# First feed-forward program of a two-block network: its tail joined to the shifted projections without a barrier, and handed over tile by tile

## The reference, cut to what matters

```
# end of the first block
f = jnp.square(jax.nn.relu(h2 @ w_ff1)) @ w_ff2
x = x + g2 * rms_norm(f, g_post_ffn)
# start of the second block
xn = rmsnorm(x, norm1_g)
z = xn @ w_in
z_rwkv, u, gates = jnp.split(z, [SHIFT_COLS, SHIFT_COLS + SSM_WIDTH], axis=-1)
z_mix = z_rwkv + (token_shift(z_rwkv) - z_rwkv) * mu_shift
```

## Time and profile before

| what | us |
|---|---|
| median of three runs | 2864.79 |
| lowest and highest run | 2863.01, 2865.03 |
| profiled execution, its own time | 2850.7 |
| span of the profiled execution | 2848.9 |
| last matmul group of the down projection starts | 1221.75 |
| first matmul of product 0 starts | 1262.05 |
| first matmul of product 2 starts | 1283.93 |

### The profile page before, as it was taken

One profiled execution on the slowest core, in us unless ns is written; L12 is line 12 of the kernel. 1 busy time (PEld: TensorE's weight loads), 2 busy tenths in 40 slices (PEclk: granted clock), 3 DMA queues, 4 the chain that ended last, 5 costly groups with the idle time before them and its releaser, 6 DMA issues. The chain is left out here.

```text
span 2848.9 us, 42015 instructions
## 1 busy us (share of the span) xinstructions
PE 2725.7 (96%) x16814; PEld 2143.3 (75%) x16814; DVE 1876.4 (66%) x2843; ACT 1327.7 (47%) x1932; POOL 271.0 (10%) x429
## 2 busy tenths in 40 slices
PE   7999989999999999989999998989899999999998
PEld 4757644777888888867778887777778888888886
DVE  6678987567666466784777516665755476656676
ACT  4247756467555334453441104542324565543344
POOL 0115630001000000000000001210000110000000
PEclk9999999999999999999999999999999999999999
DMA  7721100446566888722463332207233666677884
GB/s 265 227 69 38 49 1 1 141 151 239 208 236 215 300 282 293 247 93 62 127 155 125 124 118 78 81 29 227 84 98 130 222 218 225 221 290 259 291 286 151
DMA packets 205906, 474.01 MB, mean 166 GB/s; under 512 B 49040, under 2 KB 69648, under 8 KB 199376
## 3 DMA queue, kind: packets, MB, share of 16 engines
q1 hardware_dynamic: 187792, 393.73, 41.7%
q0 software_dynamic: 17920, 77.61, 6.9%
HBM read 344.09 MB, written 124.29 MB: 164 GB/s over the span
## 5 line engine op out<-in xcount | busy, mean ns | idle before, releaser
L2126 PE MATMUL psum<-merged_operand 128*128 128x512 f32 x1536 | 360.7, 390 | 0.0
L2126 PEld LDWEIGHTS psum<-merged_operand 128*128 128x128 f32 x1536 | 288.4, 188 | 60.7
L2126 PE MATMUL psum<-h_half_operand 128*128 128x512 f32 x1344 | 316.8, 391 | 0.0
L2126 PEld LDWEIGHTS psum<-h_half_operand 128*128 128x128 f32 x1344 | 252.3, 188 | 55.5 <-issue 1.0
L2126 PE MATMUL psum<-h_half_operand,weight_parts_operand 128*128 128x512 f32 x768 | 177.4, 392 | 0.8 <-DVE weight_parts_operand L2615 0.6
L2126 PEld LDWEIGHTS psum<-h_half_operand,weight_parts_operand 128*128 128x128 f32 x768 | 143.5, 188 | 34.1 <-DVE weight_parts_operand L2615 2.7
L3573 PE MATMUL psum<-h_high,weight_high 128*128 128x512 f32 x480 | 151.8, 397 | 1.4 <-DVE h_low L228 1.4
L3573 PE MATMUL psum<-h_low,weight_high 128*128 128x512 f32 x480 | 148.1, 390 | 0.0
L3573 PE MATMUL psum<-h_high,weight_low 128*128 128x512 f32 x480 | 147.9, 389 | 0.0
L215 DVE CAST weight_high<-weight_ring 128x1024 fp32r<-128x1024 f32 (+1 forms) x54 | 31.7, 586 | 164.7 <-PE psum L3573 105.4
L2615 DVE TENSOR_TENSOR weight_parts_operand<-weight_ring,weight_parts_operand 128x1024 fp32r<-128x1024 f32 x66 | 80.7, 1223 | 85.0 <-ACT weight_parts_operand L2275 84.6
(11 more groups left out here) (645 smaller groups left out, 5935.0 us busy)
## 6 DMA issues: line engine op xcount, KB each, us to landing
o<-in_w_ff SPq DMA_DIRECT2D x80, 512.0 KB, 4.5
merged<-hidden_terms SPq DMA_DIRECT2D x56, 512.0 KB, 5.7
hidden_upper<-in_w_ff_down SPq DMA_DIRECT2D x48, 512.0 KB, 4.9
weight_ring<-in_w_out SPq DMA_DIRECT2D x32, 512.0 KB, 3.4
hidden_terms<-weight_parts POOLq DMA_DIRECT2D x16, 1024.0 KB, 7.9
hidden_terms<-weight_ring POOLq DMA_DIRECT2D x16, 1024.0 KB
hidden_upper<-in_w_ff_up SPq DMA_DIRECT2D x32, 512.0 KB, 4.6
o<-hidden_terms SPq DMA_DIRECT2D x28, 512.0 KB, 5.8
```

Source lines behind the costliest of these rows:

```text
L2126: mm = pe.matmul(bank, w[:, at:at + P], tiles(r, i), start=opens and m == 0, stop=closes and m == 2, skip_group_check=resumed)
```

## The change

The two functions now share one block, so there is no barrier between them, and the work at the seam is ordered anew:

- **Squares.** Of the four `Y_0E` squares DVE adds three into `acc_early`; PE sums `acc_early` and the fourth (`Y_0L`). The eight `X3_1` squares are no longer added by DVE: PE sums them one by one into bank 5. The sums of `X3_0` each have two small matmuls ahead of them (`idle=2`); the 28 and the 8 are gone.
- **PSUM.** DVE no longer copies banks 0 to 3; `add_second` of tiles 4 to 7 reads them where they are.
- **Slabs.** DVE splits slabs 0 and 1 right after the last matmul of the down projection, ahead of its wait for the root of bank 6, into the memory in which the head has them anyway.
- **Norm, rounding, rest.** These are done for each token half and tile: DVE makes `normed(half, t)`, ACT rounds it to `next_high`, DVE makes the rest into `next_low` (`rest_of_normed`), one tile behind. Half 1 comes first. The rounded tiles overwrite x, so ACT first waits until x of that half is stored (`later_x_stored`, `stored`).
- **Root of bank 7.** Its logarithm and exponential stand between the roundings of half 1, after tiles 3 and 5.
- **Products.** PE runs products 0 and 1 together (`first_two`): for each half and tile three matmuls for slab 0, and three for slab 1 one tile behind. From product 2 on nothing changes.

```diff
 if first:
-    sum_acc(5, acc_late, 2 * KT + 3 * OUTS)
-    sum_squares(7, X3_0)
-    K.stay_busy(pe, 4, 28)
+    sum_squares(5, X3_1)
+    sum_squares(7, X3_0, idle=2)
...
-    load_log_table(1)
-    wait(act, sq_summed, 2 * KT + OUTS)
-    root((root_x_down[:, halves[0]], 7))
+    wait(act, later_x_stored, 16)
+    for t in range(KT):
+        round_normed(1, t, t)
+        if t == 3:
+            wait(act, sq_summed, 3 * KT + 1)
+            log_of(root_x_down[:, halves[0]], 7)
+        if t == 5:
+            root_of(root_x_down[:, halves[0]])
+    wait(act, stored, 16 * KT)
+    for t in range(KT):
+        round_normed(0, t, KT + t)
...
-    for t in range(OUTS):
-        wait(dve, sq_made, begin[Y_0E] + t + 1)
-        dve.tensor_copy(tiles(y21, t), psum[:, t, :]).then_inc(c_added.sem, 1)
-    for t in range(KT):
-        add_square(X3_1, t, acc_late, t == 0)
-    wait(dve, c_added, 4 * OUTS)
+    for t in range(OUTS - 1):
+        add_square(Y_0E, t, acc_early, False)
+    wait(dve, tile_ended, tiles_by[STEPS - 1])
+    split_next_w(0)
+    split_next_w(1)
     wait_root(6)
     for t in range(KT):
         add_second(0, t, 3 * KT + t)
-    wait_root(7)
     wait(dve, dw_split, STEPS)
     wait(dve, dh_split, STEPS)
-    for t in range(KT):
-        normed(1, t)
-    wait_root(8)
-    for t in range(KT):
-        normed(0, t)
+    for half, root_at in ((1, 7), (0, 8)):
+        wait_root(root_at)
+        for t in range(KT + 1):
+            if t < KT:
+                normed(half, t)
+            if t:
+                rest_of_normed(half, t - 1, (1 - half) * KT + t - 1)
...
+def part_of_half(n, g, k):
+    cols = slice(k * P, (k + 1) * P)
+    whi, wlo = w_ahead[n]
+    for m, (w, x) in enumerate(((whi, high), (whi, low), (wlo, high))):
+        mm = pe.matmul(banks(n)[:, g, :], w[:, cols], x[:, k, at(g)],
+                       start=(k == 0 and m == 0), stop=(k == KT - 1 and m == 2))
+    if g == 0 and k == KT - 1:
+        mm.then_inc(K.slab_used.sem, 1)
+def first_two():
+    pe.wait_ge(K.slab_split.sem, split0 + 2)
+    for g in (1, 0):
+        for k in range(KT + 1):
+            if k < KT:
+                pe.wait_ge(K.tile_split.sem, tile0 + (1 - g) * KT + k + 1)
+                part_of_half(0, g, k)
+            if k:
+                part_of_half(1, g, k - 1)
...
-    K.stay_busy(pe, 7, 8)
+    first_two()
     for n in range(N):
-        product(n)
+        if n >= 2:
+            product(n)
```

More of the change, by code:

```diff
@@ L1698, in attend, with mix_and_ffn @@
             f.n += n
-def mix_and_ffn(nc, K, x_twin, room_twin, hid_twin, weights, x_from, w_up, w_down, gain, bias, first, x_dram, kept, out=None):
+def mix_and_ffn(nc, K, x_twin, room_twin, hid_twin, weights, x_from, w_up, w_down, gain, bias, first, x_dram, kept, out=None, shared_block=None):
     OUTS, MIX, PAIRS, STEPS = 4, 2 * KT, FT // 2, 56
@@ L1729, in mix_and_ffn @@
     if first:
-        SQUARES = [("PE", KT), ("DVE", KT), ("DVE", OUTS), ("DVE", OUTS), ("DVE", OUTS), ("DVE", KT), ("PE", OUTS), ("PE", KT)]
-        X2_0, X2_1, Y_0A, Y_1A, Y_1B, X3_1, Y_0E, X3_0 = range(8)
+        SQUARES = [("PE", KT), ("DVE", KT), ("DVE", OUTS), ("DVE", OUTS), ("DVE", OUTS), ("PE", KT), ("DVE", OUTS - 1), ("PE", 1),
+                   ("PE", KT)]
+        X2_0, X2_1, Y_0A, Y_1A, Y_1B, X3_1, Y_0E, Y_0L, X3_0 = range(9)
     else:
@@ L1740, in mix_and_ffn @@
             takers.append((who, counts[who]))
+    if first:
+        takers[begin[Y_0L]] = ("PE", KT + 1)
+        takers[begin[X3_1]:begin[X3_1] + KT] = [("PE", KT + 2 + t) for t in range(KT)]
     order = []
@@ L1861, in bank_b @@
             return psum[:, (2, 7)[i % 2], :]
+        loaded_next = [at + sum(16 if n < MIX else 32 for n in range(slot, SLABS, RING)) for slot, at in enumerate(loaded0)]
         def landed(n):
@@ L1911, in residual, with next_high, next_low, next_w @@
             return x[:, t, halves[h]]
-        with nc.Block() as block:
+        NORMED, AHEAD = OPERANDS + 5 + STEPS, SLABS + 2 * PAIRS + STEPS
+        def next_high(h, t):
+            return x_operand[:, t, halves[h]]
+        def next_low(h, t):
+            return hid_operand[:, 2 * t + h, :]
+        def next_w(n):
+            at = slice(n * KT * P, (n + 1) * KT * P)
+            return pair_high[:, 0:4 * HALF][:, at], pair_high[:, 4 * HALF:8 * HALF][:, at]
+        ahead_of_next = [next_w(n) for n in range(2)] if first else None
+        with nc.Block() if shared_block is None else nullcontext(shared_block) as block:
             @block.sync
@@ L2114, in sum_acc, with sum_squares @@
                     sum_of(bank, of).then_inc(summed.sem, 1)
-                def sum_squares(bank, group, begins=True):
+                def sum_squares(bank, group, begins=True, idle=0):
                     many = SQUARES[group][1]
@@ L2257, in load_log_table, with log_of, root_of, root @@
                     act.activation(K.silu_c[:, n:n + 1], K.col("eps"), ACT.Ln)
[L2259 to L2263, removed]
-                    wait(act, log_made, len(logs))
-                    for to, _ in which:
-                        act.activation(to, to, ACT.Exp, scale=-0.5).then_inc(root_made.sem, 1)
+                def log_of(to, bank):
+                    logs.append(to)
+                    act.activation(to, psum[:, bank, :], ACT.Ln, scale=1.0 / D, bias=K.col("eps")).then_inc(log_made.sem, 1)
+                def root_of(to):
+                    wait(act, log_made, len(logs))
+                    act.activation(to, to, ACT.Exp, scale=-0.5).then_inc(root_made.sem, 1)
+                def root(which):
+                    log_of(*which)
+                    root_of(which[0])
+                def round_normed(h, t, count):
+                    wait(act, h_made, 2 * KT + count + 1)
+                    act.activation(next_high(h, t), hid_b[:, 2 * t + h, :], ACT.Copy).then_inc(pair_rounded.sem, 1)
                 def round_source(half, k):
@@ L3396, in _ @@
                                                    op1=ALU.add))
-                split_w(0)
-                for k in range(KT):
-                    rest_of_tile(dve, K, xhigh0, k, normed, high, low)
-                split_w(1)
                 dve.wait_ge(K.load_done.sem, load0 + 32)
```

102 lines of the change are left out of this document (59 added, 43 removed).

## The result

In the first comparison the changed kernel took 2842.1 us (median of four runs, 2839.9 to 2849.8) against 2863.9 us of the kernel before (four runs, 2861.9 to 2865.0). The ratio of the times is 0.9947, 95% interval 0.9929 to 0.9964. So it is faster, as forecast; but 2842.1 lies under the range of 2851 to 2859, and the 21.8 us between the medians are nearly twice the 11.6 us of the sum. The two profiles show 2848.9 and 2838.5 us of span, which is 10.4 us. Before asking where further microseconds came from, the seam can be checked step by step.

A forecast was written before the change was run, and what follows sets the result against it. PE, busy 96% of the span, was taken as the bound; products 0 and 1 end 13.8 us earlier, 2.2 go back: 2850.7 - 11.6 = 2839.1 us, plus 14.1 to the runs' median gives 2853.2, range 2851.0 to 2859.0.

The forecast's parts named there:

- the sum: Whole seam: products 0 and 1 end 13.8 us earlier, 2.2 us go back, so product 2 starts 11.6 us sooner.
- The runs' median stands 14.1 us above that execution: Whole kernel: 14.1 us from profiled execution to runs' median, used to turn 2839.1 us into 2853.2 us.
- additions start: DVE's `add_second` at the seam: starts 2.3 us sooner, 5.2 us after the last down matmul, not 7.5.
- first product: PE at the seam: starts at once after the last `X3_0` sum, at 1248.3 on the old profile's clock.
- DVE's waits for ACT: Half 1 of norms and rests: logarithm and exponential of the root stall DVE by 0.7 and 0.5 us.
- idle ahead of product 2: PE between products 0 and 1 and product 2: 2.2 us idle, where it had none.
- PE was said to set its own start: Square sums ahead of the first product: PE itself is the wait; fillers cost at most 1.8 us.
- the clock rival: Low clock stretch on matmuls at the seam costs 1.5 to 3 us; time 2855 to 2856 us; chance 0.22.
- signs of being wrong: `first_two` starting after 1250 or over 24 us, gap over 4 us ahead of product 2, or changed time after it.
- what follows it is unchanged and moves with it: Everything after product 2's start: takes the same time as before, only shifted with that start.
- The hand-over: Tiles passing DVE, ACT, DVE, PE: up to 3.2 us exposed; 2856 to 2857 us; chance 0.14 together with tables.
- A switch of tables: ACT's root: 1.31 us a switch; rival form, twice that, gives 2856.8 us; chance 0.14 together with hand-over.

The follow-up runs named there:

- a lag of three: Changed kernel with product 1 three tiles behind product 0 instead of one; mean 2845.0 us over 11 executions, product 2 after 50.88 us.
- late splits: Changed kernel with the splits of slabs 0 and 1 behind the additions to x and ahead of the norms; mean 2848.7 us, product 2 after 54.58 us.

## Why the prediction was right and wrong

**The step that failed** is the last sentence of the sum: "The runs' median stands 14.1 us above that execution; taking the gain off it gives 2853.2 us", and with it "the median itself moves by about 1". The 14.1 us are no fixed distance between a profiled execution and a run. Over 86 later executions the kernel before spread from 2846.9 to 2864.9 us, with the granted clock: the profiled one lies at the low end of that, the three runs at the high end (their clocks are not on record). The mean of the 86 is 2856.5 us, 5.8 us above the profiled one; 2856.5 - 11.6 is 2844.9, and the changed kernel's mean over 20 is 2845.5. With the shown median as an anchor the forecast was 8.3 us too high. The other 2.8 us down to the measured 2842.1 are the four executions of the changed kernel, which lay 3.4 us under the mean of the 20, against 0.6 us by which that mean is above 2844.9. The three runs lay within 2 us of each other, and the profile's own time stood 14 us below: that contradiction was in the times shown, and should have widened the range downward. The 21.8 us of the first comparison are the same effect: 11.0, and 7.4 by which the kernel before's median was above its later mean, and 3.4 by which the changed one's was below. 11.0 us, give or take 2.1, is the size over all executions, 11.4 the seam. One thing is not explained: all four executions of the kernel before in the first comparison took 2861.9 us or more, and only 6 of the 86 later ones did. As four independent draws that would be very rare, so something that no run here shows may have held them up.

**The steps of the seam**, forecast and measured, each from the last 24 down matmuls:

| step | forecast | measured |
|---|---|---|
| additions start | 10.9 | 10.91 |
| first norm | 22.9 | 22.90 |
| first product | 26.6 | 26.17 |
| DVE's waits for ACT | 0.7, 0.5, none | 0.69, 0.36, 0.38 |
| idle ahead of product 2 | 2.2 | 2.07 |
| product 2 | 50.6 | 50.80 |

The first product was in truth as late as forecast. Its record starts at 1246.99 while the last sum, started at 1246.53 and 0.86 us long, is still under way until 1247.39, which is 26.6 us after the down matmuls; the product's second matmul starts at 1247.63. From there to the last start at 1269.17 it is 21.5 us for 94 steps, 0.2 us more than at 0.227 each. Most of that is one wait for a tile (the pair at 1258.77 takes 0.78 us, its neighbours 0.62), and it follows the third wait for ACT, which the forecast did not have. Product 2 is 0.2 us late by it.

**PE was said to set its own start.** It does, but that was worth nothing: without fillers it starts 0.69 us sooner and product 2 doesn't move, because PE then waits for tiles. PE is nowhere more than about 1.5 us behind DVE's tile, and at 1258.77 it has caught up. The runs with a lag of three and with late splits show the other side of that: there DVE set the pace.

**The rivals.** The clock did not drop between the down matmuls and product 2 in any of the three profiles of the changed kernel. But right behind the gap of 2.07 us it fell in one of the three, on matmuls, and cost 1.6 us, which is what the clock rival said (1.5 to 3 us). The forecast and this rival thus both occur, from execution to execution; neither explains the miss, which has the other sign. Of the prediction's signs of being wrong one came true, the changed time behind product 2 (1.9 us in the first pair of profiles): "what follows it is unchanged and moves with it" holds for the instructions, not for their time. The clock did matter for the whole: the spread follows it, and the fillers, which the forecast costed at up to 1.8 us of loss, go with a gain of 5.3 us, give or take 2.5. The hand-over was hidden nearly as forecast: 1.4 us of waits on DVE, about 0.2 us of them on PE. A switch of tables cost 1.30 us (1248.52 to 1249.82) and no more. The Trainium skill, "ScalarE: Activation LUTs", section "What ACT_TABLE_LOAD costs", says about 2.66 us with the drain, and this trace disagrees. The barrier's removal by itself was not tried, since the barrier keeps the reused memory apart.

**What stays open.** Why the executions differ in their clock at all, and why without the fillers more of them are long while the seams in both of those profiles are as short as with them. Long and short profiled executions alike show low stretches in the recurrence, where no kernel here has other instructions than another; those that take longer behind product 2 mostly have more of them there. Why the kernel before was so slow in the first comparison is open too. No profile of the kernel before above 2851.5 us was caught.

## What to carry to other kernels

When a profiled execution and the timed runs disagree by more than the gain that is forecast, the level of the time is unknown: forecast the difference from the trace, and give the level a range that holds both. Work on two weight slabs at once while the operand arrives tile by tile: at 1.27 us a tile from DVE, one slab left PE idle for 0.3 us at each and cost 6.2 us, two filled it. Where two products end together, the next one waits for the drain of the first; letting the second lag only in its last tiles shortened that wait from 2.07 to 0.69 us and brought product 2 forward by 1.1 us, while a lag from the start gave it all back. And read the profile past the point where the gap ends: what a gap costs can lie in the matmuls behind it (1.6 us here, in three of seven profiles).

## What the runs showed of the hardware

86 executions of one unchanged program on one core lay between 2846.9 and 2864.9 us, with mean granted clocks from 0.982 to 0.988, and the time followed the clock by about 2 us for each 0.001. Sixteen filler calls, 3.7 us of PE time that moved the first product by 0.7 us and product 2 by nothing, went with a mean clock of 0.9864 in place of 0.9845 and with 5.3 us less time over a program of 2850 us. The same idle time of 2.07 us ahead of the same matmuls was followed by the clock at 0.50 in three profiles and by 1.00 in four; 2.29 us ahead of the square sums by 0.50 in one and 1.00 in the other.
